# Earlier order of three weight splits, the gate arithmetic and two clears ahead of a mixture-of-experts stage

## The reference

```python
h = h + hgrn2_mixer(rms_norm(h, hgrn_norm[j]), ..., hgrn_w_out[j], layer)
h = h + moe_swiglu(rms_norm(h, moe_norm[j]), moe_w_router[j], moe_w_gate[j], moe_w_up[j], moe_w_down[j])

def moe_swiglu(u, w_router, w_gate, w_up, w_down):
    t = u.reshape(B * S, D)
    logits = (t @ w_router).astype(F32)
    top_vals, top_idx = lax.top_k(logits, TOP_K)                 # 2 of 8 experts
    top_w = jax.nn.softmax(top_vals, axis=-1)
    gates = jnp.sum(jax.nn.one_hot(top_idx, N_EXPERTS, dtype=F32) * top_w[..., None], axis=1)
    out = jnp.zeros((B * S, D), F32)
    for e in range(N_EXPERTS):
        y = swiglu_2(t, w_gate[e], w_up[e], w_down[e]).astype(F32)   # D = 1024, expert width 3584
        out = out + gates[:, e:e + 1] * y
```

## Time and profile before

| | us |
|---|---|
| median of 3 runs | 2200.31 (2200.22 to 2202.57) |
| the profiled execution's own time | 2202.57 |
| its span, from first to last instruction | 2200.8 |
| PE busy | 2151.7 (98%) |
| DVE busy | 1411.9 (64%) |
| ACT busy | 1182.2 (54%) |
| POOL busy | 43.6 (2%) |

### The profile page before, as it was taken

How to read it: one execution, slowest core, us unless ns; L and a number is a source line. 1 busy time by engine, 2 the same in 40 slices (tenths; PEclk the granted TensorE clock), 3 DMA queues, 4 the chain that set the end, 5 groups by cost and what they waited for, 6 DMA issues and landing times.

```text
span 2200.8 us, 26591 instructions
## 1 busy us (share of the span) xinstructions
PE 2151.7 (98%) x10426; PEld 1754.3 (80%) x10426; DVE 1411.9 (64%) x1193; ACT 1182.2 (54%) x1107; POOL 43.6 (2%) x94
## 2 busy tenths in 40 slices
PE   7999999999999999999998999999999999999998
PEld 7757889868888758889876888888888888888887
DVE  1425444455444735542725888888888988888887
ACT  1335432444433534432533777767776777767775
POOL 1001000010000000000000000000000000000000
PEclk9999999999999999999997999999999999999999
DMA  7325554545554225555324999999999999999996
GB/s 251 115 77 191 190 183 149 186 172 191 190 174 144 96 77 201 191 185 162 123 96 156 359 347 361 370 338 374 340 363 350 358 347 360 371 337 374 341 363 256
DMA packets 208179, 539.60 MB, mean 245 GB/s; under 512 B 10045, under 2 KB 67486, under 8 KB 208110
## 3 DMA queue, kind: packets, MB, share of 16 engines
q1 hardware_dynamic: 204224, 530.61, 68.4%
q0 software_dynamic: 2096, 7.87, 1.1%
q10 hardware_dynamic: 1790, 0.14, 0.1%
HBM read 537.54 MB, written 1.05 MB: 245 GB/s over the span
## 4 chain that ended last, share of the span: by engine, by line
PE 90%; ACT 5%; issue 2%; DVE 2%; DMA 1%; POOL 1%; DVEq 0%; SPq 0%; ACTq 0%; POOLq 0%
PE ps L1962 12%; PE ps L1964 12%; PE ps L1963 12%; PE ps L509 11%; PE ps L622 5%; PE ps L624 5%; PE ps L623 5%; PE ps L586 5%; PE ps L527 4%; ACT ring_r L1953 3%; PE ps L663 3%; PE ps L665 3%; PE ps L664 3%; PE ps L1972 2%; PE ps L2017 1%
## 5 line engine op out<-in xcount | busy, mean ns | idle before, releaser
L1958 DVE TENSOR_TENSOR ring_r<-ring,ring_r 128x2048 fp32r<-128x2048 f32 x339 | 761.9, 2287 | 97.7 <-ACT ring_r L1953 97.7
L1953 ACT ACTIVATE ring_r<-ring 128x2048 fp32r<-128x2048 f32 x339 | 630.8, 1912 | 57.3 <-DMA ring<-in_moe_w_gate 46.5
L1962 PE MATMUL ps<-ring_r,arena_r 128*128 128x512 f32 x1344 | 532.2, 396 | 1.0 <-DVE arena_r L2190 1.0
L1964 PE MATMUL ps<-ring_r,arena_r 128*128 128x512 f32 x1344 | 524.9, 391 | 0.0
L1963 PE MATMUL ps<-ring_r,arena_r 128*128 128x512 f32 x1344 | 524.8, 391 | 0.0
L324 DVE TENSOR_TENSOR ring_r<-ring,ring_r 128x2048 fp32r<-128x2048 f32 x99 | 226.9, 2292 | 234.4 <-ACT ring_r L315 234.4
L1964 PEld LDWEIGHTS ps<-ring_r,arena_r 128*128 128x128 f32 x1344 | 253.0, 188 | 54.7
L1962 PEld LDWEIGHTS ps<-ring_r,arena_r 128*128 128x128 f32 x1344 | 253.2, 188 | 51.8 <-issue 1.2
L1963 PEld LDWEIGHTS ps<-ring_r,arena_r 128*128 128x128 f32 x1344 | 253.4, 189 | 50.4
L315 ACT ACTIVATE ring_r<-ring 128x2048 fp32r<-128x2048 f32 x99 | 189.4, 1917 | 182.1 <-DMA ring<-in_ffn_w_up 81.9
L509 PE MATMUL ps<-arena,ring 128*128 128x128 f32 (+1 forms) x1600 | 261.5, 324 | 4.3 <-ACT arena L368 2.7
(11 more groups left out here) (322 smaller groups left out, 1800.0 us busy)
## 6 DMA issues: line engine op xcount, KB each, us to landing
ring<-in_moe_w_gate SPq DMA_DIRECT2D x115, 1024.0 KB, 5.3
ring<-in_moe_w_up SPq DMA_DIRECT2D x112, 1024.0 KB, 5.3
ring<-in_moe_w_down SPq DMA_DIRECT2D x112, 1024.0 KB, 5.0
ring<-in_ffn_w_gate SPq DMA_DIRECT2D x33, 1024.0 KB, 5.1
ring<-in_ffn_w_up SPq DMA_DIRECT2D x33, 1024.0 KB, 5.2
ring<-in_ffn_w_down SPq DMA_DIRECT2D x33, 1024.0 KB, 4.9
ring<-in_attn_w_in SPq DMA_DIRECT2D x24, 1024.0 KB, 5.4
ring<-in_hgrn_w_in SPq DMA_DIRECT2D x16, 1024.0 KB, 5.5
```

What stands on the lines that cost most here:

```text
L1953: nc.scalar.activation(unit_parts(k)[0], ring[:, slot_of(k), 0:2048], ACT.Copy).then_inc(m_hi, 1)
L1958: nc.vector.tensor_tensor(low, ring[:, slot_of(k), 0:2048], high, ALU.subtract).then_inc(m_lo, 1)
L1962: nc.tensor.matmul(out_, x[:, 0, f, :], w[0], start=first, stop=False)
L1964: return nc.tensor.matmul(out_, x[:, 0, f, :], w[1], start=False, stop=last)
```

## The change

On ACT the high splits of expert units 0, 1 and 2 stand in a row ahead of both `norm_sums`. On DVE the three low splits stand in a row ahead of the first `residual`. The copy of the identity and the clears of `M_selT` and `M_y` move ahead of the wait for the logits; the gate arithmetic moves from behind the selection to between `XNl` and the wait for the places. The clear of `M_cnt[:, 1:2]`, with the signal `m_yl`, stays. Nothing is added or left out.

```diff
         def M_scalar(act, step):
-            split_high(act, 0, 0)
+            for k in range(AHEAD):
+                split_high(act, 0, k)
             norm_sums(act, 7, 0)
-            split_high(act, 0, 1)
             norm_sums(act, 7, 1)
-            split_high(act, 0, 2)
             for t in range(TT):
 ...
         def M_vector(dve, step):
-            split_low(dve, 0, 0)
+            for k in range(AHEAD):
+                split_low(dve, 0, k)
             for t in range(TT):
                 residual(dve, 7, t)
-                if t:
-                    split_low(dve, 0, 1)
                 normalise_tokens(dve, 7, t)
 ...
+            nc.vector.tensor_copy(ident_r, ident[:, :])
+            nc.vector.memset(M_selT.bitcast(F32), 0.0)
+            step.link(nc.vector.memset(M_y.bitcast(F32), 0.0))
+
             dve.wait_ge(m_lg, 1)
 ...
+            dve.wait_ge(m_ex, 1)
+            step.link(nc.vector.tensor_scalar(M_w[:, 0], M_w[:, 1], 1.0, None, ALU.add))
+            step.link(nc.vector.reciprocal(M_w[:, 0], M_w[:, 0]))
+            step.link(nc.vector.tensor_tensor(M_w[:, 1], M_w[:, 1], M_w[:, 0], ALU.mult))
+            for k, onehot in enumerate((OH0, OH1)):
+                ins = nc.vector.tensor_tensor(onehot, onehot, M_w[:, k].to_broadcast([P, TT, NE]), ALU.mult)
+            step.link(ins)
+            step.link(nc.vector.tensor_tensor(GATE, OH0, OH1, ALU.add))
             dve.wait_ge(m_pos, 1)
 ...
             select(0, 0)
 ...
             nc.vector.memset(M_cnt[:, 1:2], 0.0).then_inc(m_yl, 1)
             tokens_low(0, 2)
             tokens_low(1, 4)
-            split_low(dve, 0, 2)
             with dve.Fori(0, n * NE) as i:
```

More of the change, by code:

```diff
@@ L2215, in M_vector @@
             select(0, 0)
[L2216 to L2226, removed]
             nc.vector.memset(M_cnt[:, 1:2], 0.0).then_inc(m_yl, 1)
```

## The result

The changed kernel takes 2214.23 us (median of 4 runs, 2212.74 to 2216.56), against 2201.14 us before (4 runs, 2200.22 to 2202.57). The ratio is 1.0059, with a 95% interval of 1.0042 to 1.0078: slower, by 13.1 us. The profiled execution took 2214.71 us, its span is 2212.6. The forecast was 2214.7 us, from a sum of +14.4 on the median of three runs, 2200.31.

A forecast was written before the change was run, and what follows sets the result against it. The prediction took PE as the bound (90% of the chain), with other engines setting the pace at the layer border. 10.6 + 1.1 + 1.7 + 1.0 = 14.4 us on the median 2200.31 gave 2214.7 us, range 2210 to 2219.

The forecast's parts named there:

- The cover and the gap: Layer border: tile 0's norm, formerly hidden under PE's matmuls, waits for unit 2's load and splits; PE stands still 10.6 us.
- The restart at half clock: After PE's stand: tile 0's transposes cost 1.1 us more, the last eight projection matmuls 1.7 us more.
- The row from 771 us: Earlier layer: PE resumed at 771.56 after 2.23 us of waiting; eight projection matmuls of the same shape took 5.26 us.
- Its going away gives nothing: Unit 1's low split, between tile 1's residual and normalisation, lay under ACT's and POOL's time; removing it gains nothing.
- the two ends of a spread: Residual to normalised tile: 3.47 us for tile 0 and 4.26 us for tile 1, used as bounds for the transposes' start.
- The gate arithmetic: Six DVE instructions, 1.09 us, now between `XNl` and the reduction, with 0.12 us of slack: +1.0 us.
- the clears: With the identity copy, 2.71 us moved into DVE's 3.68 us of waiting for the router: no cost.
- the prediction's own sign: The forecast would be wrong if the expert loop took another time from its first matmul to its end.
- (a): Rival, chance 0.05: PE's clock does not fall again at the border, giving back 9.2 us: +5.2, 2205.5 us.
- (b): Rival, chance 0.03: the stall before tile 0's transposes does not occur; only the gate arithmetic's +1.0 is left, 2201.3 us.
- (c): Rival, chance 0.03: the expert loop pays back five longer ACT split pieces, 23.6 us: sum -9.2, 2191.1 us.

The follow-up runs named there:

- unit 1 alone: Kernel before with only unit 1's splits (ACT and DVE) ahead of the norm of tile 0, unit 2's left in place; 2210.72 us, ratio 1.0043.
- the filled gap: Changed kernel with 23 matmuls of 256 columns, results unread, in PE's gap ahead of the transposes of tile 0; 2213.74 us, ratio 1.0059.
- splits alone: Kernel before with only the three high and three low splits ahead of the norm of tile 0; 2212.61 us, ratio 1.0051.
- ACT alone: Kernel before with the three high splits on ACT ahead of both sums of squares, DVE's order as before; 2210.51 us, ratio 1.0038.
- one split moved: Kernel before with DVE's low split of unit 1 ahead of the residual of tile 1 instead of behind it; 2200.88 us, ratio 0.9999.
- gates and clears alone: Changed kernel with the splits put back, only gate arithmetic and clears still moved; 2202.29 us, ratio 1.0005.
- the changed kernel with the long fills: Changed kernel with 23 calls of 512 columns, results unread, in the gap before the transposes of tile 0; 2222.24 us, ratio 1.0101.
- the kernel before with the short ones: Kernel before with PE's four border waits filled by 7, 5, 4 and 2 matmuls of 256 columns, results unread; 2194.22 us, ratio 0.9971.

## Why the prediction was right

**The cover and the gap (10.6 forecast, 10.13 measured).** Right, as to place and size. Unit 2's load took 5.08 us, the splits 1.92 and 2.29, all from rows. That the landing is what counts is shown by unit 1 alone (3.44 us less gap for a load 3.44 us earlier) and by the filled gap (same start of the transposes with PE busy). That ACT's queue alone suffices is shown too.

**The restart at half clock (1.1 + 1.7 forecast, 1.1 + 0.7 measured).** The mechanism was right, the second term was sized too high by 1.0. The transposes took 1.97 us as forecast. The eight projection matmuls took 4.11 us in the chain, not 5.1: the clock came back within the window 1180 to 1181 us, early in them.

```profile
1180.00:1181.00 1.00, 1.00 (x3) 0.52 (x2) 0.17 (x1) 0.00 (x0) 0.00 (x0) 0.67 0.00 0
```

The row from 771 us had the return in their last part. With other edits ahead the same eight took 4.42, 4.52 and 4.35 us (splits alone, unit 1 alone, ACT alone), against 3.60 before and 5.26 in my row, so that row was the long end and not the middle. The filled gap puts what the clock costs at 1.29 us, less than the 1.8 of the two terms. From start to start the transposes took 0.88 us before, 1.76 in the changed kernel and 1.16 in the filled gap: 0.6 us went with the clock and 0.3 stayed. That these 0.3 us are PE's wait for the second half of the tile, and the rest a matter of where a row is taken to begin, is my reading and is not shown.

**"Its going away gives nothing" (0 forecast, -0.8 measured).** This step was wrong. I took the low split of unit 1 for covered because DVE had time for it, and did not ask what it does to POOL beside it. POOL's first instruction took 1.01 us in the kernel before, from 1172.64 to 1173.65, and DVE's split ended at 1173.56; moved away, it takes 0.22. The Trainium skill, "SBUF — State Buffer", section "SBUF: two separate sides", says that a VectorE instruction with two SBUF inputs and a GpSimd instruction that reads SBUF need the same pair of ports, and that the later one is blocked until the first is done. By that rule POOL waits for the end of the split, and the trace agrees, to the 0.09 us between the two ends. That the split beside it is the cause is shown by the runs: 3.45 or 3.46 us from residual to normalised tile 1 in the four kernels named here without the split there (changed, splits alone, unit 1 alone, one split moved), 4.26 before and 4.25 with it (ACT's order alone; gates and clears alone). ACT's order is no rival, since it changed in the first of these two and 4.25 stayed. I had both numbers in the prediction and used them as the two ends of a spread, when they had a cause.

**The gate arithmetic (1.0 forecast, 0.9 measured) and the clears (0).** Right. DVE's wait for the router fell from 3.68 to 1.20 us, and still was one. The removal of 6.1 us of DVE's work ahead of the loop gained nothing: in the changed kernel DVE waited 1.45 us for ACT before its first split there.

**The rest of the run.** The sum of the measured terms is 10.13 + 1.1 + 0.7 - 0.8 + 0.9 = 12.0, and the stretch says 12.05. From the loop's first matmul to the end of the span it took 1003.97 us before and 1002.17 after, 1.8 less. By the prediction's own sign a loop of another time would have told against it, so this needs an account. Up to the first gathering inside the loop (L1972 in the chain, 1303.22 and 1316.01 us) it took 0.81 less: the loop's start at half clock ended about 1214.6 after 4.2 us, where it ended at 1202.8 after 6.0. From there to the last one (2170.38 and 2183.10) the loop took 867.16 and 867.09 us, the same. The last 0.92 lie in the tail, where the last scatter, again after a wait of 2.45 us, ran at full clock and took 1.34 less. Before and after:

```profile
2193.34 3.44 PE L1979 MATMUL ps<-arena_r,arena_r 128*128 128x512 f32 x8 [2.45 <-DVE arena_r L2212]
```

```profile
2206.05 2.10 PE L1979 MATMUL ps<-arena_r,arena_r 128*128 128x512 f32 x8 [2.45 <-DVE arena_r L2222]
```

No edit of the change touches the last scatter or the wait before it, and eleven of the traces have that wait, 2.45 us in each. Behind it the scatter took 2.10 or 2.11 us in seven, 2.61 and 2.91 in two (the changed kernel with the long fills, the kernel before with the short ones), and 3.44 in two (the kernel before, the changed kernel with its gap filled at the right length). So part of what one profile shows is the clock's timing. The two spans differ by 1.55 + 12.05 - 1.8 = 11.8 us, the medians by 13.1, and the runs of one kernel lie 2 to 4 us apart, so the border's 12 us are the part that is established. The forecast's 14.4 was 2.4 too high for it: 0.5 in the gap, 1.0 in the restart, 0.8 in POOL, 0.1 in the gates. That the forecast of 2214.7 still lies within half a us of the measured 2214.23 is luck: the median of before came out at 2201.14 instead of 2200.31, 0.8 higher, and the medians lie 13.1 apart where the border accounts for 12.05. What the prediction can claim is the place, the path and most of the size.

**The rivals.** The clock fell again as forecast (2.62 us of waiting before tile 1's transposes, clock 0.50 from 1188 on), so (a) did not come; but its sum, 9.2 us for a full clock, is borne out in size by the filled kernel, which got 7.1 in the median and 8.8 from the projection's first matmul to the end of its profile. (b) is excluded by the gap. (c) is excluded by the loop, which took the same time. Its sum was misread: the chain of before has seven pieces of 3.70 us or more on ACT's splits, not five (those were the longest), and they add to 31.0 us and not 23.6. In the changed kernel there are again seven, of 3.7 to 4.9 us, 27.4 in all, and the loop's time did not follow that difference.

## What to carry to other kernels

Before work is moved earlier in an engine's queue, look up what it waits for and when that lands: a copy of 2 us ahead of its data holds everything behind it until the data is there, and a norm that was ready 5 us before it was due came out 10 us late. Where a trace has the same steps twice with two durations, look for what ran beside the longer one before taking the two as a range. And a stretch in which PE waits several times for a few us can be slow by its clock more than by its waits; fills that ended inside the waits, or little behind them, won 7 us here, and fills of twice that length won nothing.

## What the runs showed of the hardware beyond that

- A GpSimd instruction of 0.22 us takes 1.01 us when a VectorE subtraction of two SBUF operands is running, and ends 0.09 us after it (1173.65 and 1173.56 us).
- PE's clock after a wait is not a function of the wait alone: 2.45 us before the last scatter left it at 2.10 us in seven traces and at 3.44 in two. The gathering, 7.06 us of work in a row at half clock, did not bring the clock back, while in the changed kernel it was back about 3.2 us after the transposes of tile 0 began (1177.48; 0.67 in the window 1180 to 1181, so at about 1180.7).
- A matmul of two plain fp32 operands stands in the trace as two instructions (14 for 7 calls), each 0.43 us with 512 columns and 0.22 with 256 at full clock. The projection's rows count the same way: one unit is four calls of `out_tensor` for a tile, and its row says x8.
